# Prompt attention with the next step's maxima ahead of the current combination, and scores written two steps ahead

## The reference

```
def diff_weights(scores, lam):
    p = jax.nn.softmax(scores, axis=-1)
    return p[:, :, 0] - lam * p[:, :, 1]

def one_block(args):                      # 128 queries
    s = einsum('bqhcd,bkhcd->bhcqk', qb, k) * scale
    s = where(visible, s, -inf)           # chunks of 64: key chunk <= query chunk
    return einsum('bhqk,bkhd->bqhd', diff_weights(s, lam), vf)
```

## Time and profile before

| | |
|---|---|
| Time, 3 runs | median 1456.66 us (1452.57 to 1461.25) |
| Profiled execution | 1456.57 us, span 1454.8 us |
| Busy share of the span | PE 91%, DVE 57%, ACT 39%, POOL 22% |
| Mean granted TensorE clock | 0.94 |
| Prompt attention, first mask to last block copy | 796.6 to 871.4 us |

### The profile page before, as it was taken

One profiled execution on the slowest core, in us unless ns is written; L12 is line 12 of the kernel. 1 busy time (PEld: TensorE's weight loads), 2 busy tenths in 40 slices (PEclk: granted clock), 3 DMA queues, 4 the chain that ended last, 5 costly groups with the idle time before them and its releaser, 6 DMA issues.

```text
span 1454.8 us, 23707 instructions
## 1 busy us (share of the span) xinstructions
PE 1330.3 (91%) x8072; PEld 1155.8 (79%) x8072; DVE 825.3 (57%) x1445; ACT 571.9 (39%) x1131; POOL 321.4 (22%) x276
## 2 busy tenths in 40 slices
PE   4999999999999969999996678987999999999996
PEld 2889999998778849888874345766899999988885
DVE  2666777666345464424245755238677777754545
ACT  4533443433244364232112446337344444433433
POOL 0443343432000000000101604004344444410000
PEclk9999999999999989999956578998999999999998
DMA  9545444553523323212210405002332222212232
GB/s 316 158 146 161 147 153 144 157 153 115 173 95 108 119 66 102 88 58 101 87 32 21 139 13 175 18 23 92 87 87 81 77 73 86 87 55 75 87 136 109
DMA packets 167003, 152.71 MB, mean 105 GB/s; under 512 B 10361, under 2 KB 139777, under 8 KB 166954
## 3 DMA queue, kind: packets, MB, share of 16 engines
q1 hardware_dynamic: 165610, 148.24, 32.4%
q0 software_dynamic: 1344, 3.81, 1.0%
HBM read 142.72 MB, written 9.05 MB: 104 GB/s over the span
## 4 chain that ended last, share of the span: by engine, by line
PE 79%; DVE 9%; issue 5%; ACT 4%; DMA 2%; DVEq 0%; SPq 0%; POOL 0%; ACTq 0%; POOLq 0%
PE ps L1079 75%; DVE resid L1941 1%; DVE h_sums_lo L1722 1%; DVE max_den L2216 1%; DMA resid<-in_x_sample 1%; DVE w_sums_lo L1722 1%; DMA w_raw<-in_w_ffn_in 1%; ACT probs L995 1%; DVE w_lo L1722 1%; DVE act_t L1833 1%; PE ps L1605 1%; DVE silu_gate L1826 1%; ACT x_norm L661 1%; DVE probs L2225 1%; DVE y L1904 0%
## 5 line engine op out<-in xcount | busy, mean ns | idle before, releaser
L1079 PE MATMUL ps<-h_sums_hi,w_sums_hi 128*128 128x320 f32 x1216 | 378.2, 315 | 15.2 <-ACT silu_gate L731 4.5
L1079 PE MATMUL ps<-h_sums_hi,w_sums_lo 128*128 128x320 f32 x1216 | 371.1, 309 | 0.0
L1079 PE MATMUL ps<-h_sums_lo,w_sums_hi 128*128 128x320 f32 x1216 | 371.0, 309 | 0.0
L1079 PEld LDWEIGHTS ps<-h_sums_hi,w_sums_hi 128*128 128x128 f32 x1216 | 227.1, 188 | 31.9 <-issue 20.8
L1722 DVE TENSOR_TENSOR w_lo<-w_raw,w_hi 128x512 fp32r<-128x512 f32 (+3 forms) x106 | 97.8, 923 | 232.3 <-ACT w_hi L805 157.7
L1079 PEld LDWEIGHTS ps<-h_sums_hi,w_sums_lo 128*128 128x128 f32 x1216 | 227.5, 188 | 0.0
L1079 PEld LDWEIGHTS ps<-h_sums_lo,w_sums_hi 128*128 128x128 f32 x1216 | 227.5, 188 | 0.0
L1079 PE MATMUL ps<-w_hi,act_hi 128*128 128x512 f32 x440 | 174.7, 397 | 4.3 <-issue 3.6
L1079 PE MATMUL ps<-w_hi,act_lo 128*128 128x512 f32 x440 | 172.6, 392 | 0.0
L1079 PE MATMUL ps<-w_lo,act_hi 128*128 128x512 f32 x440 | 172.5, 392 | 0.0
L1722 DVE TENSOR_TENSOR w_sums_lo<-w_raw,w_sums_hi 128x512 fp32r<-128x512 f32 x136 | 126.5, 935 | 54.3 <-ACT w_sums_hi L749 44.4
(11 more groups left out here) (325 smaller groups left out, 1919.1 us busy)
## 6 DMA issues: line engine op xcount, KB each, us to landing
w_raw<-in_w_ffn_in SPq DMA_DIRECT2D x88, 512.0 KB, 3.8
w_raw<-in_w_ada SPq DMA_DIRECT2D x28, 1024.0 KB, 5.1
w_raw<-in_w_ffn_out SPq DMA_DIRECT2D x88, 256.0 KB, 2.6
w_raw<-in_w_in SPq DMA_DIRECT2D x10, 1024.0 KB, 5.1
w_raw_start<-in_w_ada SPq DMA_DIRECT2D x8, 1024.0 KB, 7.8
w_raw<-in_w_out SPq DMA_DIRECT2D x4, 1024.0 KB, 5.0
k_cache<-in_cache_k SPq DMA_DIRECT2D x8, 512.0 KB, 4.9
v_cache<-in_cache_v SPq DMA_DIRECT2D x8, 512.0 KB, 3.8
```

The source lines that it names most:

```text
L1079: return pe.matmul(out, lhsT, rhs, start=start, stop=stop)
```

## The change

On DVE the maxima of step n+1 are written ahead of the combination of step n. Since they need their scores earlier, PE writes the scores two steps ahead: those of steps 0 and 1 at the start, and in step n those of n+2, ahead of the output products of n-1 and the transposes of n. No instruction is added or taken away, and no buffer changes; one source line is added, so that lines behind L1584 are numbered one higher.

```
             p_score(0)
+            p_score(1)
             for n in range(last_n):
-                if n + 1 < last_n:
-                    p_score(n + 1)
+                if n + 2 < last_n:
+                    p_score(n + 2)
                 if n:
                     p_out(n - 1)
                 p_transpose(n)
...
             p_maxima(0)
             for n in range(last_n):
-                p_combine(n)
                 if n + 1 < last_n:
                     p_maxima(n + 1)
+                p_combine(n)
                 if n in (4, 6):
                     grp_lo(7, (n - 4) // 2)
```

## The result

| | before | after |
|---|---|---|
| Time, 4 runs each on the same chips | median 1455.06 us (1452.57 to 1461.25) | median 1434.86 us (1432.52 to 1440.13) |
| Profiled execution | 1456.57 us, span 1454.8 us | 1432.52 us, span 1430.7 us |
| First mask of the prompt attention | 796.59 us | 790.00 us |
| Its length, first mask to end of last block copy | 74.79 us | 58.20 us |
| From there to the end of the span | 583.4 us | 582.5 us |

The ratio is 0.987, with a 95% interval of 0.984 to 0.990, so the change is worth 14 to 23 us. The forecast was 1444 us, 12.4 us less than the profiled execution; the range ended at 1438. The sign was right, and the gain was larger than forecast. The table already shows that the 24 us between the two profiles are three things: 16.6 us in the stage, 0.9 behind it, and 6.6 ahead of it, where both programs are the same.

What follows compares the result with a forecast made beforehand. Bound: a ring of DVE's maxima, ACT's exponentials and DVE's combination. Terms -16.9 + 0.9 + 1.9 + 2.5 - 0.8 = -12.4 us from 1456.57 gave 1444 us; own range 1439 to 1449, 8-in-10 range 1438 to 1451.5.

Steps and rivals of the forecast that it cites:

- PE at 1.2 GHz: Steps of 256 keys ahead of POOL's stretch and 384 keys behind it: PE slower than DVE until the clock rises, +2.5 us.
- The waits: Prompt attention, 14 of 16 steps: DVE's standstill for ACT's exponentials goes whole, -16.9 us.
- ACT in steps 0 to 3: First four steps: ACT's exponentials to squares take 2.13 us against DVE's 1.91, +0.9 us.
- GpSimd's products: Stretch where POOL's products run: eight to nine slowed DVE operations instead of seven, +1.9 us.
- The first rival: Clock stays low from 831 us on or falls back, so PE bounds the stage: 1451.5 us, chance 13%.
- The end: Last combination to end of block copy, and first sample attention transposes: PE at 2.4 GHz shortens them, -0.8 us.
- The second rival: Maxima wait for scores PE writes late, behind transposes waiting for DVE; half of 16.9 us returns: 1452.5 us, chance 6%.
- The slower rival: Shorter stage leaves TensorE at 1.2 GHz through sample attention into the output projection: 1466 us likelier, 1480 whole, chance 4%.

Runs made afterwards that it cites:

- second profile: The changed kernel run again with no edit: stage 58.09 us, median 1434.15 us, ratio 0.988 (0.986 to 0.991) to before.
- the run that awaits the end: Changed kernel with one more DVE wait, for the end of the negated, scaled maxima before the previous step's reciprocal: stage 59.20 us, 1432.05 us (one run).

## Why the prediction was right and where it was wrong

The mechanism was the one forecast, and the size was too small by about a quarter in the stage: 16.6 us for 12.4. What failed are terms of the sum: the price of PE at 1.2 GHz (+2.5, measured +0.5), the price of ACT (+0.9, measured +0.3), and a term that was put at nothing, the overlap of neighbouring instructions on DVE (measured -1.2). Every instruction of DVE in the stage is the same before and after, so their rows can be added up: durations, gaps and overlaps. Step by step:

- **The waits, -16.9.** Right: 16.9 us of waits for exponentials became none, and the run with the scores alone shows that they depend on DVE's order.
- **ACT in steps 0 to 3, +0.9.** Too large: +0.3. The length of ACT's step was right, 2.08 us for the 2.13 forecast, but DVE's own work was not 1.91 us beside it. Two of the four steps hold the maxima of 256 keys (0.69 us for the reduction instead of 0.42), and one scaling took 0.68 us instead of 0.29 while GpSimd was at work. Apart from the one wait for scores, the gaps between DVE's instructions add up to only 0.3 us more than they did before outside the waits, and with the squares moved away the four steps became 0.2 us shorter. The prediction also overlooked that step 4 has squares.
- **GpSimd's products, +1.9.** Nearly right: the durations of DVE's operations add up to 50.7 us before and 52.2 after, +1.4 (+1.9 in the second profile). There were eight slow operations, where eight or nine were forecast. That the weight subtraction and the small product can be among them I had not said.
- **PE at 1.2 GHz, +2.5.** This was the term that was mis-sized most: it cost the one wait of 0.5 us, and in the second profile of the changed kernel no wait at all. PE did fall behind about as forecast. Its transposes started at 820.37, 824.12 and 827.97 us, two steps of 3.75 and 3.85 us at 1.2 GHz against 2.74 of DVE, together 2.1 us. What the sum left out is that the scores are written two steps ahead, and that PE had its work done when GpSimd's stretch ended. The scores of steps 10, 11 and 12, and the masks that wait for them:

```profile
820.99 1.65 PE L1079 MATMUL ps<-dk_t,dq_t 64*128 64x384 f32 x4
...
824.07 0.17 DVE L2214 MEMSET ps<- 64x128 f32 x1
...
824.95 1.65 PE L1079 MATMUL ps<-dk_t,dq_t 64*128 64x384 f32 x4
...
826.82 0.17 DVE L2214 MEMSET ps<- 64x128 f32 x1
...
828.75 1.24 PE L1079 MATMUL ps<-dk_t,dq_t 64*128 64x512 f32 x4
...
830.10 0.17 DVE L2214 MEMSET ps<- 64x128 f32 x1 [0.54 <-PE ps L1079]
```

By their modelled ends, the first scores were done 1.4 us ahead of their mask and the second 0.2 us, while the third kept DVE waiting for 0.5 us; by then the clock was rising. Ahead of GpSimd's stretch the steps were held by the weight subtraction, not by PE. The first rival, 1.2 GHz to the end, did not happen. The rule of the Trainium skill ("TensorE: Matmul & The Clock Gate", "HAM oscillation — how this bites in real kernels") that would have brought it fits the stretch from 811.5 to 828, where PE was busy 8.84 of 16.5 us at a clock of 0.51. It does not fit the one behind 835 us, where PE had breaks of 0.41 to 0.74 us in every step and the clock stayed at 1.00.
- **The overlap on DVE, not in the sum.** The working counted a step of DVE from rows in which every small product is followed by a standstill. Next to an instruction that does not depend on it, it overlaps by 0.1 us. The overlaps add up to 0.3 us before and 1.5 after, so -1.2; the run that awaits the end lost 1.0 to 1.1 us.
- **The end, -0.8.** -0.7 in the stage (3.86 us for 4.57). What lies behind the stage scattered between 580.4 and 585.6 us over the profiles, so that no gain there can be claimed.

Together -16.9 + 0.3 + 1.4 + 0.5 - 1.2 - 0.7 = -16.6, which is the measured difference of the stage. The time fell by 17.3 us (13.8 to 20.9) in the repeated comparison and by 18.9 in the first. The first median, 1434.86, lies 9 us below the forecast: 4.2 us are what the sum missed in the stage, 1.6 us are the median of before, which was 1455.06 in this comparison and 1456.66 in the one that the forecast started from, and the other 3.3 are within the interval of the measurement. The range was too narrow on the low side since I had put all unknown prices on the side of a loss but one.

The second rival was wrong for this kernel and right for half of it, as the maxima alone show. The slower rival asked for 1.2 GHz in the output projection, and a part of it did happen. In the kernel before, the clock was at 1.2 GHz at the start of the sample attention and at 2.4 GHz from 905 to 915 us, ahead of the projection. In the changed kernel it was the other way round (the first row is the sample attention, the second the stretch ahead of the projection, the third the projection):

```profile
854.00:858.00 4.00, 3.93 (x60) 2.82 (x58) 2.84 (x10) 3.68 (x16) 2.10 (x2) 1.00 0.29 102
883.00:892.00 9.00, 6.59 (x41) 5.06 (x33) 3.84 (x8) 4.22 (x9) 0.00 (x0) 0.50 0.00 0
892.00:922.00 30.00, 30.00 (x154) 25.21 (x153) 6.67 (x8) 6.75 (x10) 0.00 (x0) 0.97 0.10 28
```

GpSimd's copies of the sample gates started 30.8 us behind the stage instead of 36.2, a gain of 5.4 us. The last transposes of the mLSTM heads started 47.2 us behind it instead of 48.3, so that 4.3 us of the gain were gone again. The second profile of the changed kernel gives 31.8 and 48.2. The low clock ahead of the projection is not tied to the change: it also showed in the profiles with the scores alone and with the kernel before and its products later. That the clock is what gave and took these microseconds fits the rows, but no run separates it from the rest.

## What to carry to other kernels

A ring between two engines is opened by giving one of them work that depends on neither end of the wait, but look at the third engine first: here the maxima moved alone made the kernel slower, because their scores stood behind an instruction in the same ring. When the waits are taken away, the work of the waiting engine is what remains, so measure next what stretches it; here that was a neighbour's work on GpSimd, and one wait that moved it shortened the stage by half as much as the whole reordering. For a gain of 1%, read the length of the stage between two fixed marks in each profile, since identical code ahead of it moved by up to 9 us from one execution to the next.

## What the runs showed of the hardware

- A small product on DVE that writes two columns took 0.17 us and, where a product of GpSimd ran, 1.15; the subtraction of 2048 columns took 2.28 and 3.35. Either also ran at full speed within the same stretch (0.20 and 2.28 us in the kernel before), while the reductions out of PSUM were never slower (0.96 us). The Trainium skill ("GPSIMD Engine Reference", "1. Specifications") says that GpSimd shares its SBUF interfaces with VectorE, with contention for VectorE instructions that have two SBUF inputs or run in a two-port performance mode. The subtraction has two SBUF inputs, and the trace agrees: it was slow itself in one case, and in the other GpSimd's five products beside it took 8.49 us instead of 6.33. The small product has one, and no row shows in which mode it ran.
- A slowed operation of DVE took 0.9 to 1.1 us more whatever its size, less than the 1.27 us of one product of GpSimd (6.33 us for five). GpSimd paid too. Five products took 8.42 us (and those 8.49) where a weight subtraction lay beside them, and 6.17 with nothing beside them that slowed them; the difference is about the 2.28 us of a subtraction. That fits an engine that waits until the other's instruction is over; no run here tests it by itself.
- The granted clock in the same code, from 760 to 780 us, was 0.50 in one execution and 0.67 in another.
- Two neighbouring instructions of DVE with no wait between them overlapped by 0.1 us; with a wait for the first one's end the second started 0.04 us behind that end.
